# The four sums of the down projection's weights, on GpSimd instead of VectorE

## The reference

```
def half_step_ffn(x, g_pre, g_post, w_gu, w_down):
    h = rms_norm(x, g_pre)
    gate, up = jnp.split(h @ w_gu, 2, axis=-1)
    y = (jax.nn.silu(gate) * up) @ w_down
    return x + 0.5 * rms_norm(y, g_post)
```

## Time and profile before

| | us |
|---|---|
| median of 3 runs | 1889.91 (1889.72 to 1893.48) |
| the profiled execution | 1892.27 |
| its span, first to last instruction | 1890.5 |
| TensorE matmuls, busy | 1869.0 (99%) |
| VectorE, busy | 1368.6 (72%) |
| ScalarE, busy | 802.8 (42%) |
| GpSimd, busy | 35.0 (2%) |

### The profile page before, as it was taken

One profiled execution on the slowest core, in us unless ns is written; L12 is line 12 of the kernel. 1 busy time (PEld: TensorE's weight loads), 2 busy tenths in 40 slices (PEclk: granted clock), 3 DMA queues, 4 the chain that ended last, 5 costly groups with the idle time before them and its releaser, 6 DMA issues.

```text
span 1890.5 us, 36316 instructions
## 1 busy us (share of the span) xinstructions
PE 1869.0 (99%) x14337; PEld 1826.6 (97%) x14337; DVE 1368.6 (72%) x2127; ACT 802.8 (42%) x1278; POOL 35.0 (2%) x27
## 2 busy tenths in 40 slices
PE   8999999999999999999999999999999999999997
PEld 8999999999999999998898899999999999999997
DVE  7876766766666885578888668986776667756784
ACT  6423232323445673146565646523232223354553
POOL 0000000000000000000101100000000000000000
PEclk9999999999999999999999999999999999999999
DMA  5253433344898783210100464243434433599775
GB/s 190 79 190 122 148 129 137 132 164 142 269 294 259 221 267 111 61 43 25 36 31 30 140 243 168 87 171 124 144 122 161 150 129 139 171 303 294 227 239 181
DMA packets 115308, 296.60 MB, mean 157 GB/s; under 512 B 13137, under 2 KB 44761, under 8 KB 110329
## 3 DMA queue, kind: packets, MB, share of 16 engines
q1 hardware_dynamic: 115048, 294.93, 45.8%
q10 hardware_dynamic: 144, 0.03, 0.0%
HBM read 221.25 MB, written 73.00 MB: 156 GB/s over the span
## 4 chain that ended last, share of the span: by engine, by line
PE 92%; DVE 4%; ACT 1%; issue 1%; DMA 1%; SPq 1%; DVEq 0%; ACTq 0%
PE PS L654 9%; PE PS L656 9%; PE PS L655 9%; PE PS L763 7%; PE PS L765 7%; PE PS L764 7%; PE PS L663 5%; PE PS L664 5%; PE PS L665 5%; PE PS L886 2%; PE PS L887 2%; PE PS L888 2%; PE PS L627 2%; PE PS L629 2%; PE PS L628 2%; PE PS L1077 2%
## 5 line engine op out<-in xcount | busy, mean ns | idle before, releaser
L763 PE MATMUL PS<-x_hi,w_hi 128*128 128x344 f32 x960 | 309.5, 322 | 3.7 <-DVE w_lo L2133 3.7
L765 PE MATMUL PS<-x_hi,w_lo 128*128 128x344 f32 x960 | 306.8, 320 | 0.0
L764 PE MATMUL PS<-x_lo,w_hi 128*128 128x344 f32 x960 | 306.4, 319 | 0.0
L1294 ACT ACTIVATE silu_g<-silu_g 128x344 f32<-128x344 f32 x92 | 45.0, 491 | 444.1 <-DVE silu_g L2113 259.2
L663 PE MATMUL PS<-x_hi,w_hi 128*128 128x344 f32 x640 | 204.6, 320 | 0.0
L664 PE MATMUL PS<-x_lo,w_hi 128*128 128x344 f32 x640 | 204.2, 319 | 0.0
L665 PE MATMUL PS<-x_hi,w_lo 128*128 128x344 f32 x640 | 203.7, 318 | 0.0
L2140 DVE TENSOR_TENSOR x_lo<-t_raw,x_hi 128x688 fp32r<-128x688 f32 x120 | 104.0, 867 | 114.1 <-ACT x_hi L1402 113.4
L763 PEld LDWEIGHTS PS<-x_hi,w_hi 128*128 128x128 f32 x960 | 180.3, 188 | 5.8 <-DVE w_lo L2133 4.8
L764 PEld LDWEIGHTS PS<-x_lo,w_hi 128*128 128x128 f32 x960 | 180.3, 188 | 0.8
L765 PEld LDWEIGHTS PS<-x_hi,w_lo 128*128 128x128 f32 x960 | 180.2, 188 | 0.0
(11 more groups left out here) (311 smaller groups left out, 4438.9 us busy)
## 6 DMA issues: line engine op xcount, KB each, us to landing
raw<-in_w_gu SPq DMA_DIRECT2D x88, 512.0 KB, 4.3
t_raw<-spill_h SPq DMA_DIRECT2D x238, 172.0 KB, 2.9
raw<-in_w_down SPq DMA_DIRECT2D x152, 256.0 KB, 3.6
d_raw<-in_w_down SPq DMA_DIRECT2D x44, 512.0 KB, 6.2
spill_s<-d_sum SPq DMA_DIRECT2D x22, 1024.0 KB, 5.2
raw<-spill_s SPq DMA_DIRECT2D x88, 256.0 KB, 4.5
spill_h<-T SPq DMA_DIRECT2D x22, 688.0 KB, 3.1
spill_h<-h_odd SPq DMA_DIRECT2D x22, 516.0 KB, 2.7
```

The costliest lines, as they stand in the source:

```text
L763: nc.tensor.matmul(PS[:, bank, :GW], hi[:, c], vh, start=opens, stop=False, skip_group_check=again)
L764: nc.tensor.matmul(PS[:, bank, :GW], hi[:, c], vl, start=False, stop=False, skip_group_check=again)
L765: mm = nc.tensor.matmul(PS[:, bank, :GW], lo[:, c], vh, start=False, stop=closes, skip_group_check=again)
```

## The change

The four sums leave VectorE's pairs and the down projection's fourth block pair. GpSimd runs a loop over the 11 steps before its work for the mixer, and again behind it. Each step waits for the two loads (`d_in`) and for the store of the sums before (`sums_out`). The sums count on a semaphore of their own, `down_made`; `made` counts only the four token sums, and its constants are halved. The first credit on `sums_out` is given by GpSimd instead of VectorE.

```
+            def down_sums(f):
+                for i in range(FFN_STEPS):
+                    n = 4 * (FFN_STEPS * f + i)
+                    pool.wait_ge(S["d_in"], 32 * (FFN_STEPS * f + i) + 32)
+                    pool.wait_ge(S["sums_out"], 16 * (FFN_STEPS * f + i) + 16)
+                    nc.gpsimd.tensor_tensor(d_sum[:, W_S1], d_raw[0][:, HALF:], d_raw[1][:, HALF:], ALU.add).then_inc(S["down_made"], 1)
+                    nc.gpsimd.tensor_tensor(d_sum[:, W_S3], d_raw[0][:, 0:HALF], d_raw[0][:, HALF:], ALU.subtract).then_inc(S["down_made"], 1)
+                    pool.wait_ge(S["down_made"], n + 1)
+                    nc.gpsimd.tensor_tensor(d_sum[:, W_S2], d_sum[:, W_S1], d_raw[0][:, 0:HALF], ALU.subtract).then_inc(S["down_made"], 1)
+                    pool.wait_ge(S["down_made"], n + 3)
+                    nc.gpsimd.tensor_tensor(d_sum[:, W_S4], d_raw[1][:, 0:HALF], d_sum[:, W_S2], ALU.subtract).then_inc(S["down_made"], 1)
...
-                    sp.wait_ge(S["made"], 8 * (done + i) + 8)
+                    sp.wait_ge(S["down_made"], 4 * (done + i) + 4)
                     sp.dma_start(sums[i], d_sum[:]).then_inc(S["sums_out"], 16)
...
-                    if t == 0 and not first:
-                        down_sums(i - 1)
                     if second:
-                        down_sums(i - 1)
                         h_sums(i, 0)
...
-                behind = {2: lambda: h_sums(PAIR_STEPS, 1), 3: lambda: down_sums(PAIR_STEPS), 13: u2, 24: v, 30: c22, 35: c12, 37: lambda: fold(("F", b, 2)),
+                behind = {2: lambda: h_sums(PAIR_STEPS, 1), 13: u2, 24: v, 30: c22, 35: c12, 37: lambda: fold(("F", b, 2)),
```

More of the change, by code:

```diff
@@ L344, in build @@
  "pTs_done s_attc_done "
- "dve_seq cleared vecs_in w0_half x0_in x0_low y_gained y_half_scaled x_half_new x1_low "
+ "down_made dve_seq cleared vecs_in w0_half x0_in x0_low y_gained y_half_scaled x_half_new x1_low "
  "p_done p_read part_copied s_sum s_high s_low xn_done xs_done xs_high xs_low xp_high xp_low "
@@ L402, in t_out @@
                 def t_out(i):
-                    sp.wait_ge(S["made"], 8 * (done + i) + 4)
+                    sp.wait_ge(S["made"], 4 * (done + i) + 4)
                     sp.dma_start(hd[i][:, T1:SPILLS], T[:]).then_inc(S["t_out"], 16)
@@ L1213, in _ @@
             nc.gpsimd.memset(eps[:], EPS).then_inc(S["ones_done"], 1)
+            pool.sem_inc(S["sums_out"], 16)
+            def down_sums(f):
[9 more added lines that the diff above has]
+                    nc.gpsimd.tensor_tensor(d_sum[:, W_S4], d_raw[1][:, 0:HALF], d_sum[:, W_S2], ALU.subtract).then_inc(S["down_made"], 1)
+            down_sums(0)
             pool.wait_ge(S["x_new"], NG)
@@ L1246, in _ @@
             low_attention(2)
+            down_sums(1)
         @block.scalar
@@ L1821, in _ @@
             dve.sem_inc(S["w_ready"], READY_CREDIT)
-            dve.sem_inc(S["sums_out"], 16)
             dve.wait_ge(S["vecs_in"], 16)
@@ L1985, in h_sums @@
                 def h_sums(i, t):
-                    n = 8 * (FFN_STEPS * f + i)
+                    n = 4 * (FFN_STEPS * f + i)
                     if t == 0:
@@ L1998, in h_sums @@
                     nc.vector.tensor_tensor(T[:, 3], h_odd[:, 1], T[:, 1], ALU.subtract).then_inc(S["made"], 1)
[L2000 to L2010, removed]
                 for g in range(NG):
@@ L2087, in pair @@
                     dve.wait_ge(S["odd_out" if t else "even_out"], 16 * (FFN_STEPS * f + i))
-                    dve.wait_ge(S["made"], 8 * (FFN_STEPS * f + i) - 4)
+                    dve.wait_ge(S["made"], 4 * (FFN_STEPS * f + i))
                     nc.vector.tensor_tensor(hs[:, 2], part, PS[:, 5, :GW], ALU.add).then_inc(S["p_read"], 1)
```

## The result

The changed kernel takes 1894.44 us (median of 20 runs, 1892.98 to 1895.92) against 1890.99 us of the kernel before (20 runs, 1889.17 to 1893.48): 3.45 us more, ratio 1.0018, 95% interval 1.0012 to 1.0024. The profiled execution has a span of 1893.6 us against 1890.5. The forecast was +3.0 us with a time of 1892.9; of the 1.5 us between this and the measured time, 1.1 us is the median of before, which was 1889.91 over the first three runs.

What follows compares the result with a forecast made beforehand. TensorE, never idle in the first FFN loop, was taken as the bound, with only VectorE's lateness at single points mattering. Removal 0, steady steps 0, two openings 2 x 1.5: 1889.91 + 3.0 = 1892.9 us, range 1889.5 to 1899.5.

Steps and rivals of the forecast that it cites:

- The bound: Whole kernel: VectorE's busy time is not the bound, only its lateness at single points; at most 3.7 us to gain.
- Removal at 0: Steady steps and last step: taking the four sums off VectorE, 61 us over 22 steps, changes the time by 0.
- The turns: Where both engines read SBUF: one waits until the other's instruction is through, some 1.1 us per sum of 512.
- the openings: First steps of each half-step, VectorE crowded: 1.5 us lost per opening, +3.0 us for two, bounds 1.6 and 4.2.
- The steady step: 16 steps in the FFN loops: L2110 0.57 us late, its margin 0.86 down to 0.29 us, cost 0.
- The second step of the openings: Next loads landing at 98.7 us: second `s_lo` held, 0.7 us lost; early landing 0, late 1.3.
- Nothing meets: Rival, all sums: engines clash only where VectorE has a faster mode, so the sums vanish; 1889.9 us, chance 0.12.
- GpSimd keeps its turn: Rival, 18 steps: GpSimd's next sum precedes waiting VectorE, L1983 waits for all four; about 1925 us, chance 0.04.
- The freed VectorE closes gaps: Rival, down projection: all four TensorE waits for L2133 vanish; 1886.2 us at best, chance 0.04.
- The fourth sum falls in front of the weight remainder: Rival, 16 steady steps: L1910 precedes sum 4, L1827 held 1.15 us; 5.6 us more, 1898.5 us, chance 0.20.

Runs made afterwards that it cites:

- memsets: Changed kernel with GpSimd's four sums replaced by four 128x512 memsets at the same place (not the layer): 1889.96 us, ratio 0.9996 to the kernel before.
- the fifth sum: Changed kernel with the first sum made twice, five GpSimd sums per step: 1912.1 us, ratio 1.0111 to the kernel before.
- the last experiment: SyncE's last-step h_odd and T sends one block pair later: 1888.2 us on the kernel with the first two steps' sums late, 1887.91 on the kernel before.

## Why the prediction was right

**The bound.** TensorE was full, and stayed full in the loop. The sign and the size (+3.0 forecast, +3.45 measured, interval 1.2 to 2.4 thousandths) came from counting how much room single results have.

**Removal at 0.** Held: with memsets the sums are gone from both engines, and the time isn't told from that of before. One place was misread: in the last step the sums stood behind the fourth block pair, not between the third and the fourth. VectorE then sat idle for 3.3 us ahead of the fifth pair's low parts, so the 0 stands.

**The turns.** Held. The 1.1 us of a hold, read off three meetings in the mixer's stage, fits the first step of the openings: I had the second `s_lo` 0.8 us late; the product that reads it starts 0.69 us late in the first half-step and 0.84 in the second.

**The steady step.** Held, with 0.39 us of room where I had 0.29. `s_lo` and L1925 were held for 0.46 and 0.47 us where I had 0.5 and 0.57. GpSimd's second sum, which waits in each of these steps, has a median of 1.73 us, where I had medians near 1.3 for all four. That the room was thin is shown by the fifth sum: 0.60 to 0.84 us per step.

**The second step of the openings.** Here the path was wrong, and that the size came out near is luck. I put the landing of the second pair of loads at 98.7 us and the loss of 0.7 us on the second `s_lo`, at 109.5, and I had an early landing cost 0. GpSimd began at 97.86, near the early bound of 97.7, and the step lost 1.08 us, not 0. The loss came earlier, through `w_lo` and L2110, at the product at 103.5 where I had counted none. I had let sums 1 and 2 fall on L1910 and L1827 (it was sums 2 and 3), but followed the lateness to the second `s_lo` only; L2110 stands behind L1827 here as in the steady step.

```profile
99.37 1.40 DVE L1925 TENSOR_TENSOR h_odd<-h_odd,silu_g 128x344 f32<-128x344 f32 x1
100.69 2.31 DVE L1842 TENSOR_TENSOR w_lo<-raw,w_hi 128x1024 fp32r<-128x1024 f32 x1
102.92 0.50 DVE L2110 TENSOR_TENSOR h_odd<-h_odd,PS 128x344 f32<-128x344 f32 x1
```

L1925 and `w_lo` are each held, some 2 us together. L2110's room before was 0.96 us:

```profile
100.56 0.50 DVE L2110 TENSOR_TENSOR h_odd<-h_odd,PS 128x344 f32<-128x344 f32 x1
...
102.02 0.32 PE L654 MATMUL PS<-x_hi,w_hi 128*128 128x344 f32 x1
```

The three weight sums behind them were held for 0.2 us only, and `s_lo` came in time. In the second half-step the holds fell later: L2110 cost 0.43 us, the weight sums were held for 1.2 us, and the product on the second `s_lo` lost 0.25. So my path was there too, at a third of its size. Both openings together: 3.3 us by the starts, 3.8 with the slower start behind each wait, against the 3.0 of the sum.

**The rivals.** "Nothing meets" fell with the first VectorE record of the opening: by the note of the Trainium skill that names only VectorE's 2-port modes (Advanced Engine Details and Errata, VectorE Performance Modes) these operations would not have met. The wider sentence of the Trainium skill (GPSIMD Engine Reference, Key points) holds for two SBUF inputs, with 2.30 instead of 1.22 us for `w_lo`. "GpSimd keeps its turn" fell: the longest of all 160 records of L1998 is 1.78 us, one hold and not several. "The freed VectorE closes gaps" is excluded by the memsets and by the last experiment. "The fourth sum falls in front of the weight remainder" did not happen in a steady step with four sums; with five the last one did.

## What to carry to other kernels

Work moved to an idle engine wasn't free here: the two engines, both reading SBUF, held each other. Look at which of the other engine's results have little room, and put the moved work where none of them is queued. Here the same 88 sums cost 3.4 us at the place where their data happened to land, and nothing that can be measured once 16 of them stood behind one more semaphore wait. And ask first what the full engine waits for: two stores and their waits moved by one place in SyncE's list were worth 3 us, the 60 us of relief on VectorE nothing.

## What the runs showed of the hardware

The opening said that the engines meet only at semaphores; VectorE and GpSimd also meet where both read SBUF. A wait between them shows as no idle time on either engine, only as a longer record (L1998: median 0.69, longest 1.78 us). In the openings, with both queues full, one instruction of each went in after the other. In the mixer's stage, GpSimd's memset beside VectorE's fold (0.96 us) and the 0.53 us memsets here lengthened no VectorE record.

A wait of 2 us may cost more than itself: behind the two waits of 2.4 and 1.9 us in the one trace of five sums the granted clock was 0.52 and 0.51 for some 3 us. Behind the waits of the changed kernel's openings, all up to 1.1 us, it stayed at 1.00:

```profile
92.00:96.00 4.00, 4.00 (x28) 4.00 (x27) 2.23 (x4) 1.61 (x5) 0.00 (x0) 1.00 0.97 310
1257.00:1260.00 3.00, 3.00 (x21) 3.00 (x20) 2.22 (x2) 0.74 (x3) 0.71 (x1) 1.00 0.45 185
```

That the waits lowered it is likely and not shown. The kernel before has a stretch at the lower level in the mixer, where TensorE's records leave no gap in the 19 us ahead of it (in the stretch below the granted clock is 0.72 on average); the changed kernel has one at the same place.

```profile
1089.00:1095.00 6.00, 6.00 (x35) 0.72 0.70 281
```
